# A two-layer network on one NeuronCore: the last group of the two later FFN down products as seven block products, the root table loaded ahead of each norm, and ten matmuls of zeros at the start

## What is computed

```python
def rms_norm(x, gain):
    xf = x.astype(jnp.float32)
    y = xf * lax.rsqrt(jnp.mean(xf * xf, axis=-1, keepdims=True) + EPS)
    return (y * gain.astype(jnp.float32)).astype(x.dtype)

def swiglu_ffn(h, w_gate_up, w_down):        # D_FF_2 = 2816
    gate, up = jnp.split(h @ w_gate_up, 2, axis=-1)
    return (jax.nn.silu(gate) * up) @ w_down
```

## Time and profile before

| | us |
|---|---|
| median of three runs (1700.11 to 1700.25) | 1700.16 |
| the profiled execution | 1700.47 |
| its span, first to last instruction | 1698.6 |
| mean granted clock of TensorE | 1.000 |
| TensorE busy, matmuls | 1678.5 (99%) |
| VectorE, ScalarE, GpSimd busy | 927.7, 701.3, 685.4 |
| DMA, mean over the span | 112 GB/s |

### The profile page before, as it was taken

One profiled execution on the slowest core, in us unless ns is written; L12 is line 12 of the kernel. 1 busy time (PEld: TensorE's weight loads), 2 busy tenths in 40 slices (PEclk: granted clock), 3 DMA queues, 4 the chain that ended last, 5 costly groups with the idle time before them and its releaser, 6 DMA issues.

```text
span 1698.6 us, 22530 instructions
## 1 busy us (share of the span) xinstructions
PE 1678.5 (99%) x8690; PEld 1385.2 (82%) x8690; DVE 927.7 (55%) x1619; ACT 701.3 (41%) x1193; POOL 685.4 (40%) x320
## 2 busy tenths in 40 slices
PE   8999999999999999999999999999999999999999
PEld 6887888888888788789888888899766888888887
DVE  3877899677966759433551451148784427226211
ACT  3433254244244655434332342276864333333221
POOL 4333202403303232534475484424722255845842
DMA  9522235453545468314413413322201251341332
GB/s 252 101 75 75 75 113 162 116 160 120 171 124 155 134 227 288 102 62 124 145 42 112 149 49 104 92 80 71 75 1 39 74 161 62 99 141 58 99 100 74
DMA packets 241833, 189.60 MB, mean 112 GB/s; under 512 B 40512, under 2 KB 198848, under 8 KB 241728
## 3 DMA queue, kind: packets, MB, share of 16 engines
q1 hardware_dynamic: 239856, 182.79, 35.8%
q10 hardware_dynamic: 1872, 5.37, 1.0%
HBM read 168.73 MB, written 19.40 MB: 111 GB/s over the span
## 4 chain that ended last, share of the span: by engine, by line
PE 88%; DVE 7%; ACT 3%; issue 1%; DMA 0%; DVEq 0%; SPq 0%; ACTq 0%
PE ps L420 15%; PE ps L422 14%; PE ps L421 14%; PE ps L448 7%; PE ps L450 6%; PE ps L449 6%; PE ps L662 3%; PE ps L664 3%; PE ps L665 3%; PE ps L542 2%; PE ps L544 2%; PE ps L543 2%; PE ps L1048 1%; PE ps L1078 1%; DVE x_rows L2071 1%
## 5 line engine op out<-in xcount | busy, mean ns | idle before, releaser
L1275 POOL TENSOR_TENSOR w_lo<-w_raw,w_hi 128x1024 fp32r<-128x1024 f32 (+2 forms) x224 | 542.4, 2437 | 906.8 <-ACT w_hi L1455 869.8
L420 PE MATMUL ps<-a_hi,w_hi 128*128 128x512 f32 (+1 forms) x1184 | 442.1, 373 | 0.0
L421 PE MATMUL ps<-a_lo,w_hi 128*128 128x512 f32 (+1 forms) x1184 | 440.4, 372 | 0.0
L422 PE MATMUL ps<-a_hi,w_lo 128*128 128x512 f32 (+1 forms) x1184 | 440.3, 372 | 0.0
L1455 ACT ACTIVATE w_hi<-w_raw 128x1024 fp32r<-128x1024 f32 (+3 forms) x263 | 265.3, 1030 | 123.5 <-DMA w_raw<-in_ffn_w_gate_up_dram 43.1
L420 PEld LDWEIGHTS ps<-a_hi,w_hi 128*128 128x128 f32 x1184 | 223.0, 188 | 40.3 <-issue 1.9
L422 PEld LDWEIGHTS ps<-a_hi,w_lo 128*128 128x128 f32 x1184 | 223.0, 188 | 38.5
L421 PEld LDWEIGHTS ps<-a_lo,w_hi 128*128 128x128 f32 x1184 | 223.1, 188 | 38.4
L2615 DVE TENSOR_TENSOR ev<-ps,xh 128x512 f32<-128x512 f32 x44 | 30.4, 692 | 324.9 <-PE ps L422 293.6
L448 PE MATMUL ps<-w_hi,a_hi 128*128 128x512 f32 (+1 forms) x288 | 112.4, 390 | 1.0 <-DVE a_lo L1977 1.0
L450 PE MATMUL ps<-w_hi,a_lo 128*128 128x512 f32 (+1 forms) x288 | 111.4, 387 | 0.0
(11 more groups left out here) (390 smaller groups left out, 2817.5 us busy)
## 6 DMA issues: line engine op xcount, KB each, us to landing
w_raw<-in_ffn_w_gate_up_dram SPq DMA_DIRECT2D x88, 512.0 KB, 3.7
w_raw<-in_w_up_dram SPq DMA_DIRECT2D x44, 512.0 KB, 3.9
w_raw<-in_ffn_w_down_dram SPq DMA_DIRECT2D x28, 512.0 KB, 3.5
w_raw<-in_w_in_dram SPq DMA_DIRECT2D x20, 512.0 KB, 4.5
w_raw<-in_w_down_dram SPq DMA_DIRECT2D x20, 512.0 KB, 3.9
s_records<-stage SPq DMA_DIRECT2D x16, 544.0 KB, 5.3
w_raw<-in_ssm_w_glu_dram SPq DMA_DIRECT2D x16, 512.0 KB, 4.5
side_raw<-in_ffn_w_down_dram SPq DMA_DIRECT2D x16, 512.0 KB, 6.2
```

Source lines behind the costliest of these rows:

```text
L420: pe.matmul(bank, wh, xh_, start=first, stop=False)
L421: pe.matmul(bank, wh, xl_, start=False, stop=False)
L422: return pe.matmul(bank, wl, xh_, start=False, stop=last)
L1275: pool.tensor_tensor(lo, raw, w_hi[:, n % RING, 0:w].bitcast(F), ALU.subtract).then_inc(lo_made, 1)
```

## The change

It has four parts. (1) All three groups of f2 and f3 use block products. The last group has six feature tiles, so each product takes a chunk of two pairs and a chunk of one pair (`kns`). Its first four products run as before; then m3 runs for token tile 0 and tile 1, and m7 and m4 run for tile 0 and then for tile 1 (`by_tile`). In f2 the norm's tiles 0 and 1 are turned between them (`turn_between`), tile 2 after them. VectorE's adds of m3, m7 and m4 are spread over the norm's adds (`add_last_fast`); ScalarE asks for a chunk after each tile. (2) `root_table` takes a root of one element ahead of each rms norm and of mix0, so that the table load is done there. (3) VectorE writes 128 x 512 zeros first and TensorE runs ten matmuls of them ahead of the first turn of x. (4) SyncE's final stores follow the new order of the banks.

```diff
+WARM = 10
         def is_fast(stage, g):
-            return stage != "f1" and g < FAST
+            return stage != "f1"
...
-            def fast_rows(stage, g, w, f0, base):
+            def fast_rows(stage, g, w, f0, f1, base, turn=None):
+
+                kns = (2, (f1 - f0) // 2 - 2)
...
+                def block_part(name, block, chunk, bank, i, t, first):
+
+                    wh, wl = chunk
+                    o = opened[bank][t]
+                    x = slice(t * P, t * P + P)
+                    for kk in range(kns[i]):
+                        end = i == 1 and kk == kns[i] - 1
+                        ah, al = (a[:, 2 * i + kk, BLOCKS[block], x] for a in (hs_hi, hs_lo))
+                        pe.matmul(o, ah, wh[:, kk, :], start=(first and i == 0 and kk == 0), stop=False,
+                                  skip_group_check=not first)
+                        pe.matmul(o, ah, wl[:, kk, :], start=False, stop=False, skip_group_check=not first)
+                        m = pe.matmul(o, al, wh[:, kk, :], start=False, stop=end, skip_group_check=not first)
...
+                def by_tile(order, after=None):
+
+                    chunks = {}
+                    for t in range(2):
+                        for name, block, weights, bank, reread in order:
+                            if reread is not None:
+                                pe.wait_ge(chain_read, reads + reread + t + 1)
+                            for i in range(2):
+                                if t == 0:
+                                    chunks[name, i] = block_chunk(weights, i)
+                                m, over = block_part(name, block, chunks[name, i], bank, i, t, reread is None)
+                                if t and i == 0:
+                                    chunk_over(m)
+                            if t:
+                                chunk_done.append(over)
+                            if after:
+                                after(name, t)
+
+                def turn_between(name, t):
+
+                    if (name, t) == ("m7", 0):
+                        pass_bank()
+                        pass_bank()
+                        turn(0)
+                    if (name, t) == ("m4", 0):
+                        turn(1)
+                    if (name, t) == ("m4", 1):
+                        pass_bank()
+                        pass_bank()
 
                 product("m1", "a11", "b11", "chain", 1)
                 product("m2", "a12", "b21", "first", 2)
                 product("m6", "s2", "t2", "chain", 3, reread=0)
                 product("m5", "s1", "t1", "second", 3)
+                if g == len(GROUPS_2) - 1:
+                    open_pair("third")
+                    by_tile([("m3", "n4", "b22", "second", 4)])
+                    by_tile([("m7", "s3", "t3", "chain", 2), ("m4", "a22", "t4", "third", None)],
+                            turn_between if turn else None)
+                    return
...
+            pe.wait_ge(zeros_made, 1)
+            for _ in range(WARM):
+                pe.matmul(ps[:, 7, :], zeros[:, 0:P], zeros[:, :], start=True, stop=True)
...
+            def root_table():
+
+                step(act.activation(eps_c[:, 3:4], eps_c[:, 1:2], ACT.Sqrt))
+
             def rms_and_split(stage, added, ready, dst, chunks=0):
 
+                ahead(chunks_at[added(0)])
+                root_table()
                 deviation(stage, added, ready, 0)
                 for t in range(TT):
-                    if t == 2:
-                        make(chunks)
+                    if t and chunks:
+                        make(chunks + t)
                     if t + 1 < TT:
                         deviation(stage, added, ready, t + 1)
                     split_tile(stage, t, dst)
...
-            added = lambda t: ("f2", "down", 2, 1, t)
-            rms_and_split("mla", added, bank_ready(added), to_a, chunks_at[("kv_a", 0)] + 3)
+            added = lambda t: ("f2", "fast", 2, "m3" if t < 2 else "m4", t % 2)
+            rms_and_split("mla", added, bank_ready(added), to_a, chunks_at[("kv_a", 0)])
...
+            v.memset(zeros[:, :].bitcast(F), 0.0).then_inc(zeros_made, 1)
...
+            def add_last_fast(stage):
+
+                k = n_fast[0] - 1
+
+                def add(t):
+                    if t == 0:
+                        last[0:2] = add_m3(k)
+                    if t >= 2:
+                        add_m7(k, t - 2)
+                        last[t] = add_m4(k, t - 2)
+                return add
```

More of the change, by code:

```diff
@@ L34 @@
 GROUPS_2 = ((0, 8), (8, 16), (16, 22))
-FAST = 2
 PAIRS = 4
@@ L639, in fast_rows, with block_chunk @@
                 reads = 6 * len(fast_groups)
-                fast_groups.append((stage, g, len(chunk_src), rows))
+                fast_groups.append((stage, g, len(chunk_src), rows, kns))
                 opened = {}
-                def product(name, block, weights, bank, ready, reread=None):
+                def block_chunk(weights, i):
+                    src = {"b11": (0, 0), "b21": (1, 0)}.get(weights)
+                    if src:
+                        return take_chunk(rows(src[0], i, src[1]), kns[i], HALF)
+                    return take_chunk(None, kns[i], HALF, side=SIDE[weights] + i)
@@ L654, in product @@
+                def product(name, block, weights, bank, ready, reread=None):
+                    open_pair(bank)
+                    for i in range(2):
+                        chunk = block_chunk(weights, i)
+                        pe.wait_ge(lo_ready, base + 3 * (2 * i + kns[i] - 1) + ready)
                         for t in range(2):
@@ L656, in product @@
                                 pe.wait_ge(chain_read, reads + reread + t + 1)
[L657 to L668, removed]
+                            m, over = block_part(name, block, chunk, bank, i, t, reread is None)
                         if i == 0:
@@ L1406, in _ @@
                     load_attention_constants()
-            for half in range(2):
+            for bank, r, half in (("first", 0, 0), ("second", 0, 1), ("chain", 1, 1), ("third", 1, 0)):
                 c = slice(half * HALF, half * HALF + HALF)
-                for t in range(TT):
-                    sp.wait_ge(*freed[bank_no[("f3", "down", len(GROUPS) - 1, half, t)]])
+                for t in range(2 * r, 2 * r + 2):
+                    sp.wait_ge(*freed[bank_no[("f3", "fast", len(GROUPS_2) - 1, bank, t % 2)]])
                     sp.dma_start(out[0, t * P:t * P + P, c], x_rows[:, t, c]).then_inc(o_out, 16)
@@ L2591, in add_fast, with add_m3 @@
+            def add_m3(k):
+                return [add_block(k, "m3", t, 0, 1, ALU.add, wait=2, last_of="second") for t in range(2)]
+            def add_fast(k):
+                add_first(k)
                 for t in range(2):
[L2592 removed]
+                    add_m7(k, t)
+                add_m3(k)
                 for t in range(2):
[L2594 to L2596 removed]
@@ L2597, in add_fast @@
[L2597 to L2606 removed]
+                    add_m4(k, t)
```

100 lines of the change are left out of this document (54 added, 46 removed).

## The result

The changed kernel takes 1690.74 us (median of four runs, 1690.65 to 1691.21) where the kernel before takes 1700.13 (1699.78 to 1700.25): 9.4 us or 0.55% less, ratio 0.9945 with a 95% interval of 0.9933 to 0.9958. The forecast was 1691.5, range 1687.9 to 1695.0.

What follows compares the result with a forecast made beforehand. TensorE, busy for 1678.5 of 1698.6 us, was taken as the bound. Gains of 3.06 (start), 0.7 (root table), 1.23 (f2) and 3.63 (f3) sum to 8.6 us, giving a median of 1691.5 us, range 1687.9 to 1695.0.

Steps and rivals of the forecast that it cites:

- Start: Before the first product: zeros raise TensorE's clock early; twelve matmuls save 2.40, second turns 0.37, earlier split 0.29: 3.06 us.
- Rival (a): At the start, the clock doesn't rise earlier despite the zeros: 3.1 us more, 1694.6 us; chance 0.17.
- Root table: Ahead of f2's FFN, the early table load saves 0.7 us; nothing in the norm after the first FFN.
- f2: Last group and norm: 4.08 us from fewer matmuls and 0.9 from an old wait, less 3.75 new waits: 1.23 us gained.
- old wait for the second tile: In the norm behind f2, the new order removes this wait, 0.8 us and its restart 0.1.
- m3 behind m5: In both new groups, m3 adds to m5's bank directly behind it: a new wait of 0.35 us with the weights' reload.
- turning of tile 2: Behind f2, its bank is freed 6.7 us after m4's tile 0, against 5.4 on TensorE: 1.35 us wait.
- last key and value chunks: Behind f2, the last chunk loads only as m7's tile 1 frees a slot: 0.4 us more.
- The two starts of the groups: In f2's and f3's last groups, side chunk ready 7.6 us after first product G, wanted at G+8.2: no wait.
- Rival (b): Side chunks start as late as in the older groups: 2.6 us in each stage, 1696.7 us; chance 0.10.
- rival (d): GpSimd becomes the bound if short chunks cost 2.38 us: 4.3 more in each stage, 1704.1 us; chance 0.03.
- f3: Last group: 4.08 us from fewer matmuls, less 0.35 for m3's wait and 0.1 for the tail: 3.63 us gained.

Runs made afterwards that it cites:

- no_zeros: The changed kernel without the memset, TensorE's wait for it and the ten matmuls of zeros: 1694.52 us.
- zeros_5: The changed kernel with five matmuls of zeros in place of ten: 1693.16 us.
- m5_first: The changed kernel with m5 run ahead of m6 in the new groups, so m6 lies between m5 and m3: 1690.13 us.
- both: The changed kernel with the edits of m4_ahead and m5_first, and VectorE adding m7's second tile right after writing tile 2's rows: 1688.44 us.
- no_root: The changed kernel without the root of one element ahead of the norms: 1692.75 us.
- f2_plain: The changed kernel with f2's last group as the plain product and the norm's old order, root table still loaded ahead: 1691.74 us.
- twice_front: The changed kernel with GpSimd's short low halves of b11 and b21 and VectorE's short weight sums each done in two instructions: 1698.45 us.
- twice_all: The changed kernel with GpSimd doing each short low half of the new groups in two subtractions: 1703.43 us.
- m4_ahead: The changed kernel with ScalarE making both of m4's high halves before it waits for tile 0's squares behind f2: 1690.45 us.

## Why the prediction was right, step by step

**Start, 3.06 forecast, 3.3 measured.** The rise of the clock, the twelve matmuls (2.44 for 2.40), the second turns (0.42 for 0.37) and the memset's 0.48 came as worked out. The first product is 0.44 earlier instead of 0.29, since the turning of x itself is partly fast already (1.38 us for 1.94). Rival (a) is out, and `no_zeros` gives the whole of it back. One sentence was wrong. The Trainium skill (TensorE: Matmul & The Clock Gate, Part 1) has the number of slow matmuls differ between runs, and I said that the trace didn't agree, since three runs lay within 0.14 us. The runs since look as the page's rule would have them, though a profile counts the slow matmuls of one run only: the kernel before spread over 2.0 us in 39 runs (1698.95 to 1700.97), `no_zeros` over 1.1 and `zeros_5` over 1.6, while the changed kernel stayed within 0.6 in its nine runs (1690.58 to 1691.21). It isn't shown that all of the scatter is the clock's: `m5_first` and `both` start with the same ten zeros and spread over 1.5 and 1.35. Three runs were too few to set against the rule.

**Root table, 0.7 forecast, 0.8 measured** ahead of f2's FFN; 0 behind the first FFN, confirmed by `no_root`. What the prediction didn't price is its worth behind f2: it wrote the old wait of 0.9 off as "gone" with the new order, while `f2_plain` shows that it goes by the table load alone.

**f2, 1.23 forecast, 1.80 measured.** The mechanism was right, some sizes were off. Measured is the distance between starts of matmuls, less what the same matmuls take without a pause (0.227 each, 0.79 for the turning of a tile, 5.65 for the key and value product as the kernel before has it):

| term | forecast | measured |
|---|---|---|
| 18 matmuls less | -4.08 | -4.08 |
| old wait for the second tile | -0.9 | -1.15 |
| m3 behind m5 | 0.35 | 0.42 |
| m4's first low half | 1.45 | 1.28 |
| m4's short chunk | 0.2 | 0.25 |
| turning of tile 2 | 1.35 | 0.53 |
| last key and value chunks | 0.4 | 0.63 |
| slots of 0.23 to 0.30 behind each pause | none | 0.32 |

The most mis-sized term is the turning of tile 2. Its chain was put at 6.7 us from the end of m4's tile 0 (1109.63); it took 5.8:

```profile
1109.90 0.69 DVE L2651 TENSOR_TENSOR x_rows<-x_rows,ps 128x512 f32<-128x512 f32 x1 [1.15 <-PE ps L670]
...
1114.20 1.88 DVE L2651 TENSOR_TENSOR x_rows<-x_rows,ps 128x512 f32<-128x512 f32 x3
```

The idle 1.15 us ahead of the first row show that no older adds stood before it, where I had put 0.6; the steps behind it came a little closer together than I had them, since each starts before the one ahead has ended. TensorE's side was right: the second half of the turning, which alone needs that bank, could start 5.4 us behind 1109.63. The key and value term had the wrong cause. TensorE waits ahead of the second chunk (0.37) and the third (0.13), and ScalarE, which scales and copies the second from 1112.96 to 1115.3, comes to it from earlier entries of its list without an idle time, so it was ScalarE's list and not a late load. The errors go both ways, 1.2 us towards more gain and 0.7 towards less; that f2 came out within 0.6 us is partly luck.

**The two starts of the groups.** GpSimd ended its two halves at 1082.2 = G + 0.1 (forecast G + 0.6), ScalarE's copy began at G + 2.9 (forecast 2.91), and no product waited for a side chunk. Rival (b) is out, and `twice_front` shows that it would have come with a wider front. GpSimd's pair was 3.65 us (forecast 3.7), a short chunk some 1.3: rival (d) is out, and `twice_all` shows what it does once a short chunk costs 2.6.

**f3, 3.63 forecast, 3.4 measured.** GpSimd ran its ten long and short halves without making TensorE wait, the m3 wait came at 0.42 for 0.35, the tail cost 0.1, and 0.15 is in slots of 0.23 to 0.30 behind the pause:

```profile
1661.63 18.18 POOL L1333 TENSOR_TENSOR side_lo<-side_raw,w_hi 128x1024 fp32r<-128x1024 f32 x10 [5.23 <-ACT w_hi L1514]
...
1673.03 0.47 PE L667 MATMUL ps<-w_hi,hs_hi 128*128 128x512 f32 x1 [0.25 <-issue]
```

The sum was 1.2 us short in the profile: 0.6 of it f2, 0.3 the start, 0.4 between the first FFN and the norm behind it, 0.2 ahead of f2's group, less 0.2 in f3 (each rounded). Of the 0.4, 0.3 lies in that norm and stays open. In the twelve traces with zeros, no_root's among them, its third turning starts 24.9 to 25.0 us behind the FFN's last one, in the kernel before and in `no_zeros` 25.3, at the same place: VectorE's first reciprocal follows ScalarE's root of the layer norm by 0.74 us (566.00 to 566.74 in `no_zeros`) where it is 0.39 with zeros (562.67 to 563.06). So it goes with the zeros and not with the table load, but what 560 us of other work should carry over from them, the traces don't show. The two traces without it also lack the memset of zeros in VectorE's program, so the matmuls of zeros and the one instruction more on VectorE are two rivals that no run here separates.

## What to carry to other kernels

Fewer matmuls are worth their full slots only where nothing hangs on the order in which they end: the same 18 were worth 3.5 us at the end of f3 and 0.7 ahead of a norm. Before counting such a gain, list for each new wait what the other engines do in their own order, above all an engine that idles before a step while the work behind it is ready (ScalarE's 5.3 us here). A preparation (a table load, matmuls that keep the clock up) is best put in time that some other wait makes idle anyway, and sized to end with that wait.

## What the runs showed of the hardware

The place where TensorE's clock rises moves from run to run. In ten profiles with the same start, the ten zeros took 4.07 us once, 4.46 once and 4.63 or 4.64 eight times, and the turning of x took 1.25 to 1.89 us behind them; so the clock mostly rose during the turning, and the first product started between 8.10 and 8.57. The slowest of them, from `m5_first`:

```profile
5.91 1.89 PE L818 MATMUL ps<-ident,x_rows 128*128 128x128 f32 x8
8.57 0.47 PE L450 MATMUL ps<-w_hi,a_hi 128*128 128x512 f32 x1 [0.77 <-DVE a_lo L2045]
```

In none of the ten was a product slow. A low half of 512 elements took GpSimd 1.27 to 1.35 us alone and 1.80 beside VectorE, and a scaling of rows on VectorE 0.75 alone and 1.11 to 1.84 beside GpSimd: the low half doesn't run at the same time as this scaling or as VectorE's sums of weight blocks, and which of them loses depends on who started. It isn't so for all of VectorE's work: its adds of a PSUM bank took 0.69 us each beside low halves of 2.4 in the same stretch of `m4_ahead`. The Trainium skill (SBUF — State Buffer, Who interferes with whom) says of the port pair that the two engines share that whoever issues first gets it for the whole instruction and the other fully blocks, and these rows agree.
